# A two-layer hybrid decoder step: two blocks a layer with one weight stream through each, the norm's squares made tile by tile

## What is computed

```python
def rmsnorm(x, g): return x * lax.rsqrt(jnp.mean(x * x, -1, keepdims=True) + NORM_EPS) * g
def swiglu(x, w_in, w_out):
    gate, up = jnp.split(x @ w_in, 2, axis=-1)
    return (jax.nn.silu(gate) * up) @ w_out
def decoder_layer(x, ..., lp):
    x = x + 0.5 * swiglu(rmsnorm(x, lp['norm_ffn1']), lp['ffn1_w_in'], lp['ffn1_w_out'])
    proj = rmsnorm(x, lp['norm_mix']) @ lp['w_in']
    ...                      # three groups, their states in and out
    x = x + jnp.concatenate([y_rwkv, y_sc, y_ssm], -1) @ lp['w_out']
    x = x + 0.5 * swiglu(rmsnorm(x, lp['norm_ffn2']), lp['ffn2_w_in'], lp['ffn2_w_out'])
```

## Time and profile before

| | us |
|---|---|
| median of 3 runs (lowest, highest) | 1828.77 (1827.81, 1830.69) |
| the profiled execution | 1829.45 |
| its span, first instruction to last | 1827.7 |
| TensorE busy in it | 1605.3 (88%) |
| VectorE, ScalarE, GpSimd busy | 1003.6, 838.5, 639.1 |
| mean granted TensorE clock | 0.945 of full |

### The profile page before, as it was taken

The page is one execution under the profiler, slowest core; times in us unless marked ns, Lnnn a source line. Parts: engine busy times, 40 slices in busy tenths (PEclk is TensorE's granted clock), DMA queues, the critical chain, the costliest instruction groups (busy, mean ns, idle before and its releaser), DMA issues. The chain is left out here.

```text
span 1827.7 us, 41346 instructions
## 1 busy us (share of the span) xinstructions
PE 1605.3 (88%) x17389; PEld 1519.9 (83%) x17389; DVE 1003.6 (55%) x1682; ACT 838.5 (46%) x1439; POOL 639.1 (35%) x407
## 2 busy tenths in 40 slices
PE   3999979987779897999869998899786998889996
PEld 3999968985568787999869997888665887889995
DVE  3444277774668675443244433968654986554433
ACT  2544354665434554444244443547652445454531
POOL 1444323321055532444224442322212554244440
PEclk9999989998889998999969999999897999989998
DMA  4556155452044534557055561645501445265630
GB/s 141 185 184 237 64 175 152 144 167 71 3 113 124 165 118 146 184 185 242 14 191 181 183 213 55 204 129 154 155 15 29 138 130 161 71 230 185 221 126 25
DMA packets 280235, 256.28 MB, mean 140 GB/s; under 512 B 47767, under 2 KB 268285, under 8 KB 280035
## 3 DMA queue, kind: packets, MB, share of 16 engines
q1 hardware_dynamic: 275860, 251.55, 43.3%
q10 hardware_dynamic: 4190, 2.08, 0.5%
HBM read 242.22 MB, written 11.38 MB: 139 GB/s over the span
## 5 line engine op out<-in xcount | busy, mean ns | idle before, releaser
L210 POOL TENSOR_TENSOR ffn_lo<-ffn_raw,ffn_hi 128x1024 fp32r<-128x1024 f32 (+1 forms) x120 | 316.7, 2639 | 493.2 <-ACT ffn_hi L203 493.2
L203 ACT ACTIVATE ffn_hi<-ffn_raw 128x1024 fp32r<-128x1024 f32 (+1 forms) x240 | 274.9, 1149 | 384.0 <-PE ps L225 376.9
L223 PE MATMUL ps<-ffn_h_hi,ffn_hi 128*128 128x264 f32 x1408 | 404.4, 287 | 43.7 <-ACT ffn_hi L203 32.5
L224 PE MATMUL ps<-ffn_h_lo,ffn_hi 128*128 128x264 f32 x1408 | 402.4, 286 | 0.0
L225 PE MATMUL ps<-ffn_h_hi,ffn_lo 128*128 128x264 f32 x1408 | 402.1, 286 | 0.0
L223 PEld LDWEIGHTS ps<-ffn_h_hi,ffn_hi 128*128 128x128 f32 x1408 | 268.9, 191 | 44.4 <-issue 44.2
L210 DVE TENSOR_TENSOR ffn_lo<-ffn_raw,ffn_hi 128x1024 fp32r<-128x1024 f32 (+1 forms) x120 | 169.5, 1414 | 198.6 <-ACT ffn_hi L203 198.6
L224 PEld LDWEIGHTS ps<-ffn_h_lo,ffn_hi 128*128 128x128 f32 x1408 | 269.1, 191 | 0.1
L225 PEld LDWEIGHTS ps<-ffn_h_hi,ffn_lo 128*128 128x128 f32 x1408 | 267.5, 190 | 0.0
L223 PE MATMUL ps<-front_h_hi,front_hi 128*128 128x264 f32 (+1 forms) x816 | 248.8, 305 | 20.7 <-POOL front_lo L210 18.1
L210 POOL TENSOR_TENSOR front_lo<-front_raw,front_hi 128x1024 fp32r<-128x1024 f32 (+1 forms) x52 | 125.6, 2416 | 344.3 <-ACT front_hi L203 344.3
(11 more groups left out here) (360 smaller groups left out, 3122.0 us busy)
## 6 DMA issues: line engine op xcount, KB each, us to landing
ffn_raw<-in_ffn_w_in SPq DMA_DIRECT2D x88, 1024.0 KB, 6.5
front_raw<-in_w_in SPq DMA_DIRECT2D x50, 1024.0 KB, 5.2
ffn_raw<-in_ffn_w_out SPq DMA_DIRECT2D x32, 1408.0 KB, 6.2
back_sample_rows<-row_scratch SPq DMA_DIRECT2D x160, 128.0 KB, 3.0
out_raw<-in_w_out SPq DMA_DIRECT2D x16, 1024.0 KB, 5.2
sample_state<-in_state_ssm SPq DMA_DIRECT2D x8, 512.0 KB, 8.6
out_s_ssm<-sample_state SPq DMA_DIRECT2D x8, 512.0 KB, 7.5
back_sample_wkv<-in_state_rwkv_wkv SPq DMA_DIRECT2D x16, 256.0 KB, 3.4
```

Source lines behind the costliest of these rows:

```text
L203: act.activation(self.hi[n % self.RING][:, 0:k, 0:w], self._raw(n), ACT.Copy).then_inc(self.hi_ready, 1)
L210: eng.tensor_tensor(self.lo[n % self.RING][:, 0:k, 0:w], self._raw(n), self.hi[n % self.RING][:, 0:k, 0:w].bitcast(F32), ALU.subtract).the ...
L223: pe.matmul(out, hi[:, j, 0:w], x_hi[:, j], start=start and j == 0, stop=False)
L224: pe.matmul(out, hi[:, j, 0:w], x_lo[:, j], start=False, stop=False)
```

## The change

Of the 12 stages 6 remain: `load`, `front` and `back` for each layer, `fin`.

- `ffn1` becomes the first part of `front`, `ffn2` the last part of `back`. Their pieces and halves are joined to those of the projection into one `Stream`: ffn1 (68 halves) then `w_in` (51) in `front`; `w_out` (16) then ffn2 (68) in `back`. All of them now have **three** raw buffers of 8 row tiles. So `w_out` of a feed-forward block is cut in row tiles 8 + 7 + 7 rather than 11 + 11, and has 24 halves.
- The work of `vec` goes into ffn1 as `Vectors`: SyncE issues its 22 loads (the gain of ffn1 is no longer among them) behind the first three pieces, TensorE makes the transposes behind half 18, VectorE copies them out at m = 10. The gains of ffn1 and of the last norm are loaded and turned in `load`.
- `gained_input` becomes the class `Norm`, with one call for each tile. ScalarE squares tile by tile, and VectorE adds each square to the first (7 additions of 264 columns). For the norms between two joined parts the calls are placed among the additions to x. The product that follows waits for each tile of `h` rather than for all eight, and the matmul of the mean comes behind its second half, no longer its first.
- Half 0 of a `front` has its `lo` made by VectorE.
- In `front`, GpSimd's three memsets of buffers that lie over ffn1's wait until x is complete.

```diff
+    def act_square(self, act, k):
+        if self.x_ready is not None:
+            act.wait_ge(self.x_ready, k + 1)
+        act.activation(self.sq[:, k], self.env.x[:, k], ACT.Square).then_inc(self.squared, 1)
+    def dve_fold(self, dve, k):
+        ...
+        dve.tensor_tensor(self.sq[:, 0], self.sq[:, 0], self.sq[:, k], ALU.add).then_inc(self.folded, 1)
+    def pe_ready(self, pe):
+        def ready(j):
+            pe.wait_ge(self.hi_done, j + 1)
+            pe.wait_ge(self.lo_done, j + 1)
+        return ready
+FFN_PARTS = ((0, 8), (8, 7), (15, 7))
```

The end of ffn1 on ScalarE and VectorE (class `Ffn`; `following` is the norm of the projection):

```diff
+        for i, n in enumerate(range(FFN_IN, FFN_OUT)):
+            ws.split_hi(act, base + n + 4)
+            if self.following is not None and i >= 6 and i % 6 < 2:
+                self.following.act_hi(act, 2 * (i // 6 - 1) + i % 6)
+                self.following.act_square(act, 2 * (i // 6 - 1) + i % 6)
+        if self.following is not None:
+            for k in (KT - 2, KT - 1):
+                self.following.act_hi(act, k)
+                self.following.act_square(act, k)
...
+        for mt in range(KT):
+            n = base + FFN_IN + 6 * (mt // 2) + 4 + mt % 2
+            if mt % 2 == 0:
+                ws.split_lo(dve, n + 1)
+                ws.split_lo(dve, n + 3)
+            dve.wait_ge(ws.used, n + 1)
+            ...
+            dve.tensor_tensor(pr[:, mt % 2], env.ps[:, mt % 4, 0:N], rs[:], ALU.mult).then_inc(self.pr_done, 1)
+            ...
+            dve.scalar_tensor_tensor(out=env.x[:, mt], in0=pr[:, mt % 2], scalar=0.5, in1=env.x[:, mt],
+                                     op0=ALU.mult, op1=ALU.add).then_inc(self.x_added, 1)
+            if mt % 2 == 0:
+                ws.split_lo(dve, n + 5)
+            ...
+            if self.following is not None and mt % 2 == 0 and mt:
+                for k in (mt - 2, mt - 1):
+                    self.following.dve_lo(dve, k)
+                    self.following.dve_fold(dve, k)
+        if self.following is not None:
+            for k in (KT - 2, KT - 1):
+                self.following.dve_lo(dve, k)
+                self.following.dve_fold(dve, k)
```

The start of `front` on ScalarE and VectorE, and on SyncE:

```diff
+                for p in range(3):
+                    ws.load(sp, p)
+                vec.sp(sp)
...
+                for k1 in range(KT):
+                    norm1.act_hi(act, k1)
+                ws.split_hi(act, 0)
+                ws.split_hi(act, 1)
+                for k1 in range(KT):
+                    norm1.act_square(act, k1)
+                ws.split_hi(act, 2)
+                ws.split_hi(act, 3)
+                norm1.act_root(act)
+                ffn.act(act)
+                norm2.act_root(act)
...
+                for k1 in range(KT):
+                    norm1.dve_lo(dve, k1)
+                ws.split_lo(dve, 0)
+                for k1 in range(KT):
+                    norm1.dve_fold(dve, k1)
                 ws.split_lo(dve, 1)
                 ws.split_lo(dve, 3)
```

The join in `back` on ScalarE and VectorE (`OUT_HALVES` is 16, `norm3` the norm of ffn2):

```diff
-                for n in range(9, len(halves)):
+                for n in range(9, OUT_HALVES + 4):
                     ws.split_hi(act, n)
+                    if n >= OUT_HALVES - 3:
+                        norm3.act_hi(act, n - (OUT_HALVES - 3))
+                        norm3.act_square(act, n - (OUT_HALVES - 3))
...
                 for mt in range(KT):
                     if mt % 2 == 0 and mt:
                         ws.split_lo(dve, 9 + mt)
+                    if mt == KT - 1:
+                        ws.split_lo(dve, OUT_HALVES + 1)
                     dve.wait_ge(ws.used, KT + mt + 1)
                     dve.tensor_tensor(env.x[:, mt], ps[:, OUT_BANK[mt], 0:N], env.x[:, mt], ALU.add).then_inc(s("x_added"), 1)
+                    if mt:
+                        norm3.dve_lo(dve, mt - 1)
+                        norm3.dve_fold(dve, mt - 1)
```

More of the change, by code:

```diff
@@ L675, in front_stage @@
                 pieces.append([((KT, 0, 2 * P), wi[:, :, c0 + i * P:c0 + (i + 2) * P])])
-        H = len(halves)
-        ws = Stream(st, KT, pieces, halves, raw_ring=3)
+        H = len(tiles)
+        ws = Stream(st, KT, pieces, halves, raw_ring=3, on_dve={0, *range(1, len(halves), 2)})
         order = [m for kind, m in tiles if kind in ("rwkv", "tail")]
@@ L1350, in _ @@
                         pe.wait_ge(evicted, n - 2)
+                    else:
+                        pe.wait_ge(ffn.x_added, n + 5)
                     if n == 3:
                         pe.wait_ge(s("dt_in"), 1)
-                    ws.product(pe, n, ps[0:halves[n][2], n % 3, 0:N], h_hi, h_lo)
-                    if n == 0:
-                        pe_mean(pe)
+                    ws.product(pe, base + n, ps[0:halves[base + n][2], n % 3, 0:N], h_hi, h_lo,
+                               ready=norm2.pe_ready(pe) if n == 0 else None)
+                    if n == 1:
+                        norm2.pe_mean(pe)
                     more.go(n)
@@ L1460, in back_stage @@
                 pieces.append([((KT, 0, 2 * P), w_out[:, kh * KT:(kh + 1) * KT, c * 2 * P:(c + 1) * 2 * P])])
+        OUT_HALVES = len(halves)
+        ffn_pcs, ffn_halves = ffn_pieces(d["ffn2_w_in"], d["ffn2_w_out"], layer, len(pieces))
+        pieces, halves = pieces + ffn_pcs, halves + ffn_halves
         ws = Stream(st, KT, pieces, halves, raw_ring=3, buffers=(
@@ L1577, in _ @@
                         ws.split_lo(pool, 0)
-                for n in range(4, len(halves), 2):
+                for n in range(4, OUT_HALVES, 2):
                     ws.split_lo(pool, n)
+                ffn.pool(pool)
             @block.scalar
@@ L2163, in _ @@
                                ready=ready if mt == 0 else None)
+                ffn.pe(pe)
 OUTS = {
@@ L2172, with trunk @@
 }
-def trunk(nc, d, stages=("ffn1", "mix", "ffn2")):
+def trunk(nc, d):
     with ExitStack() as ctx:
@@ L2197, in trunk @@
         for layer in range(DEPTH):
[L2198 to L2204 removed]
+            mix_stages(nc, env, layer, d)
         final_stage(nc, env, d)
```

558 lines of the change are left out of this document (279 added, 279 removed).

## The result

The changed kernel takes **1799.57 us** (median of 4 runs, 1794.83 to 1803.58) against 1828.36 us for the kernel before on the same chip. The ratio is 0.9839, with a 95% interval of 0.9813 to 0.9865. That is 28.8 us saved where 46.8 were forecast; the time lies 2.6 us above the range's upper end of 1797. The profiled execution took 1803.58 us.

A forecast was written before the change was run, and what follows sets the result against it. TensorE, busy 88% of the span, was taken as the bound, with time to win at the stage ends. Six joins go from 132.8 to 86.0 us, saving 46.8: 1782.0 us forecast, 8-in-10 range 1767 to 1797.

The forecast's parts named there:

- The failed step: Start of ffn1: VectorE's folds wait for ScalarE's squares, done at 12.2 us, so half 1 starts at 14.0.
- The transposes: Start of ffn1: transposes of `vec` in ffn1's stream take 3.0 us at full clock, bounds 3.0 and 6.0.
- half-speed rival: Start of ffn1: transposes keep their 6.0 us and the clock stays low behind them; 1791 us, chance 0.13.
- the clock pays: Rival at ffn1's start: transposes keep 6.0 us, clock stays low behind them; 9.4 us more, 1791, chance 0.13.
- Squares and load: Start of ffn1: eight squares take 3.35 us, first raw piece lands 5.1 us on, longer `load` adds 0.6.
- ffn1 to the projection: Join inside `front`: 20.39 and 19.45 us become 16.0 each, including 1.0 for the clock; saved 4.4 and 3.4.
- `back` to ffn2: Join inside `back`: 17.03 and 15.25 us become 9.5 each, with a 4.1 us stop before half 15.
- the forecast chain: In `back`: `hi` of half 17 waits for its load, delaying tile 4's norm work, then `lo` of half 15; 4.1 us stop.
- The rival of a clean handover: In `back`: VectorE is 3 us earlier with half 13, so the stop vanishes; 1770 us, chance 0.17.
- Inside ffn: Feed-forward parts: extra `w_out` halves and three raw buffers cost nothing, with a load slack of 6.4 us.
- The starved stream: Rival in all four feed-forward parts: three raw buffers prefetch too little; 1843 us at a 14 us landing, chance 0.04.
- two rivals together: Low clock at ffn1's start's transposes plus no gain from ffn1 to the projection: 1799 us, chance 0.07.

The follow-up runs named there:

- the orders alone: Changed kernel with half 1's low part ahead of folds, transposes spread, low part ahead of the norm in `back`, tile 7 first before the projection: 1778.88 us, ratio 0.9720.

## Why the prediction came out high in its gain

- **The failed step is in the start of ffn1**, the time of VectorE's folds: "the last fold at 12.65, `lo` at 13.9, half 1 at 14.0". The squares were done at 28.58, which is 11.8 us from the stage's start at 16.78 and sooner than the 12.2 forecast. But the last fold ended at 15.6. Some 2 us of the 3 are one fold held by GpSimd (with GpSimd silent, the seven took 1.95 us less), the rest is the folds' own pace of 0.54. Half 1 started 17.82 us behind 15.81 where 0.6 + 14.0 were forecast. Of the 15.6 us above the forecast at the two starts, 6.2 are this lateness, 5.1 the clock behind the stop, and 4.3 the transposes and the clock behind them.
- **Its consequence was priced at nothing.** I named a "short stop before half 1", of about 1 us by my numbers (13 to 14.0), and let half 1 run at full clock. Behind a stop of 4.27 us half 1 took 5.52 us at a mean clock of 0.54 (+2.62; +2.44 in layer 1). With the stop at 2.53 us it lost 1.7, and with no stop there was no half-clock stretch behind it. At the stop of 4.1 us forecast in `back` I had added 2.0 for the clock. So this error mostly follows from the first one: the stop was sized at a quarter of what it was.
- **The transposes** cost 3.49 us against 3.0, so the half-speed rival's 6.0 was wrong on their own cost. But the clock fell behind them, which the rival "the clock pays" had: half 19 lost 1.61. Spreading them removed the fall, and cost as much.
- **Squares and load**: I took 3.35 us for the eight squares, and estimated 3.25 with a fixed cost for each; they took 2.60. Each lasts 0.41 us, but the next begins 0.31 us behind it. For the landing of the first piece I read 37.18, where ScalarE had only come free; the wait for the DMA in the changed kernel puts it at 5.2 us all the same. In layer 0 the stage started 0.97 us later, against 0.6.
- **ffn1 to the projection**: half 69 starts 6.75 us behind half 68, the forecast to the hundredth (6.83 in layer 1), and half 71 16.71 behind it against 16.0. Half 69 lost 1.58 to the clock, where 1.0 stood for the whole join, and in layer 0 half 71 lost 1.5 more.
- **`back` to ffn2**: the mechanism is shown; its sizes differ. In layer 0 the stop is 2.67 us instead of 4.1, but TensorE loses 0.6 and 1.0 in halves 10 and 12 before it, half 15 loses 1.4 to the clock and half 16 0.7. The sum comes within 0.2 of the forecast because these errors offset each other, which is luck. In layer 1 the stop is 4.58 and the sum 12.7.

```profile
690.83 1.06 ACT L203 ACTIVATE out_hi<-out_raw 128x1024 fp32r<-128x1024 f32 x1 [4.05 <-DMA out_raw<-in_ffn_w_in]
...
692.74 0.43 DVE L273 TENSOR_TENSOR ffn_squares<-ffn_squares 128x264 f32<-128x264 f32 x1
693.09 1.22 DVE L210 TENSOR_TENSOR out_lo<-out_raw,out_hi 128x1024 fp32r<-128x1024 f32 x1
...
694.45 0.56 PE L223 MATMUL ps<-y_hi,out_hi 128*128 128x264 f32 x1 [2.67 <-DVE out_lo L210]
```

These rows of the changed kernel's timelines are the forecast chain: ScalarE's `hi` of half 17 waits for the DMA, tile 4's fold comes behind it, `lo` of half 15 behind that, and TensorE waits. The rival of a clean handover was wrong for this kernel; moving the norm's work made it true.

- **Inside ffn**: the forecast held. Halves take 2.90 us at clock 1.00, and no matmul there waits for a DMA, so three raw buffers are enough. The starved stream is refuted. (Its price was also added up wrongly: by its own terms a landing at 14 us costs 44 x 2.5 us, so 1892 and not 1843.) A stretch of the changed kernel:

```profile
44.00:85.00 41.00, 41.00 (x342) 41.00 (x341) 18.33 (x30) 20.39 (x30) 17.61 (x8) 1.00 0.56 178
```

TensorE is busy 41.00 of 41.00 us.

The measured 1799.6 us is the number that the prediction gave for two rivals together, 1799. That is luck: they had 9.4 us at the transposes and 8 at the joins to the projection, and the runs show 4.3 and 3.0 there. The largest term, the late half 1 with the clock behind it (11.3), stood in neither.

What I overlooked stood in the trace of the kernel before. These are the three wide folds at the start of ffn1 with GpSimd's subtraction, then two low parts with the next, and the second of the two low parts by itself:

```profile
37.31 4.50 DVE L269 TENSOR_TENSOR ffn_norm_sq<-ffn_norm_sq 128x1056 f32<-128x1056 f32 x3 [1.36 <-ACT ffn_norm_sq L256]
38.30 2.47 POOL L210 TENSOR_TENSOR ffn_lo<-ffn_raw,ffn_hi 128x1024 fp32r<-128x1024 f32 x1 [22.08 <-ACT ffn_hi L203]
...
41.73 4.53 DVE L210 TENSOR_TENSOR ffn_lo<-ffn_raw,ffn_hi 128x1024 fp32r<-128x1024 f32 x2
41.92 3.25 POOL L210 TENSOR_TENSOR ffn_lo<-ffn_raw,ffn_hi 128x1024 fp32r<-128x1024 f32 x1 [1.15 <-ACT ffn_hi L203]
...
42.86 3.40 DVE L210 TENSOR_TENSOR ffn_lo<-ffn_raw,ffn_hi 128x1024 fp32r<-128x1024 f32 x1
```

The two low parts take 4.53 us where two of 1.22 would take 2.4. I priced single operations by the undisturbed rows, 0.43 and 1.22 us, without asking what GpSimd did beside them.

## What to carry to other kernels

- Where a VectorE operation that reads two tensors from SBUF stands on the critical path, and a GpSimd operation that also reads SBUF runs beside it, count the VectorE operation as beginning only when the other ends, or keep GpSimd out of that stretch. Here four low parts moved to VectorE at each layer's joins, at 1.2 us apiece, gave 6.8 us in all.
- When a stop of several microseconds is forecast, price the matmuls behind it at 1.2 GHz as well: the stops of 4.27 and 2.53 us here cost 2.6 and 1.7 us more behind them.
- When a queue is ordered, let what the next half needs stand ahead of what only the norm needs: the orders alone brought 20.7 us without changing an instruction's work.
- ScalarE's wait for a DMA in `back` cost nothing by itself. It cost what was queued behind it, so look at that before the DMA.

## What the runs showed of the hardware

- A VectorE operation with both inputs in SBUF that begins while a GpSimd `tensor_tensor` on SBUF runs ends behind it, by a little less than its own undisturbed length. The fold of 264 columns, 0.43 us alone, ended at 32.35, 0.29 us behind GpSimd (29.61 + 2.45 = 32.06); the fold of 528 columns above ended 0.56 us behind it (31.83 and 31.27); the low part of 1024 columns in the kernel before, 1.22 us alone, 1.09 us behind it (42.86 + 3.40 = 46.26 and 41.92 + 3.25 = 45.17). So it does its work when GpSimd is through. In `back` of the changed kernel there is a pair of another kind:

```profile
694.22 0.42 DVE L1985 TENSOR_TENSOR x<-ps,x 128x264 f32<-128x264 f32 x1
694.56 2.25 DVE L259 SCALAR_TENSOR_TENSOR ffn_h_lo<-x,cols,ffn_h_hi 128x264 fp32r<-128x264 f32 x1
...
693.63 2.89 POOL L210 TENSOR_TENSOR out_lo<-out_raw,out_hi 128x1024 fp32r<-128x1024 f32 x1 [5.08 <-ACT out_hi L203]
```

GpSimd runs from 693.63 to 696.52. The addition at 694.22 reads one input from `ps`, which is PSUM, and is not held (0.42). The one at 694.56 reads SBUF alone and ends at 696.81. GpSimd's own 2.89 us are 0.5 longer than the 2.4 that it took elsewhere (2.45 and 2.42 above), and it began while VectorE's `lo` of 693.09 ran until 694.31. The Trainium skill states this rule in "SBUF — State Buffer", section "Who interferes with whom": a VectorE instruction with two SBUF inputs contends with a GpSimd instruction that reads SBUF, and whichever comes first has the shared ports for its whole length. The traces here agree: VectorE is held where GpSimd was first, GpSimd where VectorE was, and the addition with an input in PSUM not at all (0.42 us).
- 57 small matmuls in a block, with TensorE busy throughout (31.22 of 31.22 us), were followed by 3.4 us at half clock; cut into eight parts between the halves, they were not.

```profile
93.30:96.70 3.40, 3.40 (x18) 3.40 (x17) 0.00 (x0) 0.00 (x0) 0.00 (x0) 0.50 0.91 294
```

TensorE is busy in all of that stretch of the changed kernel, at a granted clock of 0.50, that is 1.2 GHz. So the clock fell here behind work, not behind a stop. Why it did is not settled by these runs.
